# Recurrence of a two-layer hybrid trunk: one chunk's state updates on separate rows of the array, and VectorE's new states moved ahead of a weight split

## The reference, cut to what matters

```python
def _gla_chunk(S, inp):
    q, k, v, logf = inp
    b = jnp.cumsum(logf, axis=2)
    ...
    o = o.reshape(B, H, C, -1) + jnp.einsum('bhck,bhkv->bhcv', q * jnp.exp(b), S)
    b_last = b[:, :, -1]
    S_new = jnp.exp(b_last)[..., None] * S + jnp.einsum(
        'bhck,bhcv->bhkv', k * jnp.exp(b_last[:, :, None] - b), v)
    return S_new, o
```

## Time and profile before

| | |
|---|---|
| time, median of 3 runs | 2693.89 us (2693.68 to 2694.4) |
| the profiled execution's own time | 2695.14 us |
| its span, first to last instruction | 2693.3 us |
| granted TensorE clock, mean | 0.994 |
| one trip of the recurrence loop, heads 0 to 13 finished in it | 31.4 us |
| busy: PE / DVE / ACT / POOL | 98% / 66% / 48% / 15% |

### The profile page before, as it was taken

One profiled execution on the slowest core, in us unless ns is written; L12 is line 12 of the kernel. 1 busy time (PEld: TensorE's weight loads), 2 busy tenths in 40 slices (PEclk: granted clock), 3 DMA queues, 4 the chain that ended last, 5 costly groups with the idle time before them and its releaser, 6 DMA issues.

```text
span 2693.3 us, 55150 instructions
## 1 busy us (share of the span) xinstructions
PE 2649.2 (98%) x19678; PEld 2631.1 (98%) x19678; DVE 1765.3 (66%) x2908; ACT 1300.5 (48%) x2173; POOL 403.6 (15%) x792
## 2 busy tenths in 40 slices
PE   8999999999999999999999999999999999999997
PEld 8999999998999999999999999998999999999997
DVE  7888888847766534666645865548676535767644
ACT  6555666545444433444444566545444333444443
POOL 2111111101322100222200000002322101222200
PEclk9999999999999999999999999999999999999999
DMA  6444444444554555454555422344545555544553
GB/s 231 145 140 135 145 136 133 133 157 137 174 166 161 163 164 169 160 168 159 166 166 168 142 90 89 118 156 141 170 159 169 160 164 165 167 161 166 160 170 115
DMA packets 122671, 413.57 MB, mean 154 GB/s; under 512 B 13856, under 2 KB 20160, under 8 KB 122592
## 3 DMA queue, kind: packets, MB, share of 16 engines
q1 hardware_dynamic: 114480, 406.37, 47.2%
q10 hardware_dynamic: 7056, 3.21, 0.4%
q0 software_dynamic: 1056, 2.92, 0.3%
HBM read 406.97 MB, written 5.48 MB: 153 GB/s over the span
## 4 chain that ended last, share of the span: by engine, by line
PE 96%; DVE 3%; ACT 1%; issue 0%; DMA 0%; DVEq 0%; SPq 0%; ACTq 0%
PE bank L231 30%; PE bank L233 30%; PE bank L232 30%; DVE X L1126 1%; DVE Y L1123 1%; PE bank L1681 1%; PE bank L806 1%; DVE h_lo L1110 1%; DVE w_lo L225 1%; PE bank L767 1%; PE bank L774 0%; PE bank L807 0%; DVE Y L1140 0%; PE bank L1686 0%; ACT w_hi L218 0%
## 5 line engine op out<-in xcount | busy, mean ns | idle before, releaser
L231 PE MATMUL bank<-h_hi,w_hi 128*128 128x288 f32 (+1 forms) x4208 | 1266.4, 301 | 22.5 <-DVE h_lo L1110 13.5
L225 DVE TENSOR_TENSOR w_lo<-raw,w_hi 128x1024 fp32r<-128x1024 f32 (+2 forms) x786 | 955.2, 1225 | 453.7 <-ACT w_hi L218 453.2
L232 PE MATMUL bank<-h_lo,w_hi 128*128 128x288 f32 (+1 forms) x4208 | 1252.6, 298 | 0.0
L233 PE MATMUL bank<-h_hi,w_lo 128*128 128x288 f32 (+1 forms) x4208 | 1248.9, 297 | 0.0
L218 ACT ACTIVATE w_hi<-raw 128x1024 fp32r<-128x1024 f32 (+2 forms) x786 | 808.0, 1037 | 852.3 <-PE bank L233 846.7
L231 PEld LDWEIGHTS bank<-h_hi,w_hi 128*128 128x128 f32 x4208 | 792.9, 188 | 28.2 <-issue 22.6
L233 PEld LDWEIGHTS bank<-h_hi,w_lo 128*128 128x128 f32 x4208 | 796.4, 189 | 0.2
L232 PEld LDWEIGHTS bank<-h_lo,w_hi 128*128 128x128 f32 x4208 | 794.7, 189 | 0.6
L1295 POOL TENSOR_TENSOR ext<-yt,small 128x256 f32<-128x256 f32 x176 | 213.0, 1210 | 1507.4 <-ACT yt L1181 1036.1
L231 PE MATMUL bank<-g_hi,w_hi 128*128 128x288 f32 x1408 | 416.8, 296 | 0.0
L232 PE MATMUL bank<-g_lo,w_hi 128*128 128x288 f32 x1408 | 415.4, 295 | 0.0
(11 more groups left out here) (251 smaller groups left out, 2034.7 us busy)
## 6 DMA issues: line engine op xcount, KB each, us to landing
raw<-in_w_fi SPq DMA_DIRECT2D x352, 512.0 KB, 4.0
raw<-in_w_hi_in SPq DMA_DIRECT2D x128, 512.0 KB, 4.0
raw<-in_w_fo SPq DMA_DIRECT2D x128, 512.0 KB, 3.5
raw<-in_w_fo SPq DMA_DIRECT2D x64, 384.0 KB, 3.3
raw<-in_w_ho SPq DMA_DIRECT2D x32, 512.0 KB, 4.1
raw<-in_w_mo SPq DMA_DIRECT2D x32, 512.0 KB, 3.8
raw<-in_w_down SPq DMA_DIRECT2D x18, 512.0 KB, 4.5
raw<-in_w_ukv SPq DMA_DIRECT2D x16, 512.0 KB, 3.7
```

Source lines behind the costliest of these rows:

```text
L225: dve.tensor_tensor(w_lo[:, ch.slot, 0:n], raw[:, ch.slot, 0:n], w_hi[:, ch.slot, 0:n].bitcast(F32), ALU.subtract).then_inc(lo_done, 1)
L231: pe.matmul(out, w_hi[:, ch.slot, w], rhs_hi, start=start, stop=False)
L232: pe.matmul(out, w_hi[:, ch.slot, w], rhs_lo, start=False, stop=False)
L233: return pe.matmul(out, w_lo[:, ch.slot, w], rhs_hi, start=False, stop=stop)
```

## The change

The products for the third block are restricted to the rows that hold keys: rows 0 to 63 for the prompt, rows 64 to 95 for the sample. The fourth product writes columns 384 to 511 of bank `GS` in place of `SU`, and L614 reads it there. This holds for heads 0 to 14; head 15's updates stay as they are. In the loop, VectorE's `new_states` moves from behind `lo(5)` to before it. The order in the end functions is unchanged.

```diff
@@ new_states
             dve.scalar_tensor_tensor(out=s_new[:, 1, :], in0=s_old[:], scalar=HG.EB[:, T - 1:T],
-                                     in1=su[:, 3 * P:4 * P], op0=ALU.mult, op1=ALU.add)
+                                     in1=(GS if su is SU else su)[:, 3 * P:4 * P], op0=ALU.mult, op1=ALU.add)
@@ hgrn_dve
                 gates_keys_queries(dve, r)
-            lo(5)
             if tail:
                 new_states(dve, t)
+            lo(5)
             if main:
                 decay_sums(dve, r)
@@ updates
-            for n in range(NB + 1):
-                up = pe.matmul(su[:, n * P:(n + 1) * P], ktok[0:BL, n, :], vtok[0:BL, min(n, NB - 1), :], start=True, stop=True)
+            if su is SU:
+
+                rows = [(SU, 0, slice(0, BL)), (SU, 1, slice(0, BL)), (SU, 2, slice(0, 64)), (GS, 3, slice(64, BL))]
+            else:
+                rows = [(su, n, slice(0, BL)) for n in range(NB + 1)]
+            for bank, n, part in rows:
+                up = pe.matmul(bank[:, n * P:(n + 1) * P], ktok[part, n, :], vtok[part, min(n, NB - 1), :], start=True, stop=True)
             up.then_inc(S["updates"], 1)
```

## The result

The changed kernel takes 2699.56 us in the median of 15 runs (2698.78 to 2700.08), the kernel before 2694.59 us in 15 runs (2693.68 to 2696.54). The ratio is 1.0019, 95% interval 1.0012 to 1.0025: 5.0 us or 0.19% slower, just inside the 0.2% that the prediction took for no change, yet with an interval that leaves 1 out. The span of the profiled execution goes from 2693.3 to 2698.3 us at the same granted clock of 0.994.

A forecast was written before the change was run, and what follows sets the result against it. TensorE, busy for 98% of the span, was taken as the bound. The move's -2.5 us plus 8.6 for three changes of size gave +6.1, from 2693.89 to 2700.0 us; range 2692.8 to 2701.3, the forecast's own 2698.8 to 2701.3.

The forecast's parts named there:

- rivals with pairs: In `updates`, the third and fourth products run at once: -0.25 us in sum with the move, 2693.6; chance 0.34.
- part of the price: In `updates`, the fourth product's weights load while the third streams: 0.10 less per head, +4.6 us, 2698.5; chance 0.06.
- Three changes of size, no overlap: In `updates`, TensorE stops entering the third product, entering the fourth and leaving: +0.575 us a head, +8.6; chance 0.54.
- The price of a change: Around the narrow products, idle time plus a weight load with nothing over it: 0.20 us per entry, 0.175 for leaving.
- the way out: From the narrow products to L762's transposes: a stop plus a weight load estimated at 0.75 x 0.10, 0.175 us a head.
- The wait of the outputs: At L774, waiting for L620's states costs 0.21 us a head in twelve heads; the move removes it: -2.5 us.
- The sum of the two parts: The move's -2.5 us plus 8.6 for the third block on separate rows gives +6.1 us, median 2700.0.
- `lo(5)` and its transfer, late by 1.1 us, cost nothing: In the loop, `lo(5)` ends at 268.4 instead of 267.26; covers of 4.5 us for `mm(5)`, 9 us for the transfer.
- The states don't wait for the updates: In VectorE's `new_states`: updates end 1.17 us before L604, delayed by 0.50 at most; the rival wait got no chance.
- What would show it: Signs: no L620 waits at L774, three PEld idle times of 0.17 us, L767 to L762 1.40, trip about 31.77.
- The rules weighed: For `updates`: changing tiling mode drains TensorE (three changes, the choice), or weight loads overlap across differing row groups (pairs).

The follow-up runs named there:

- e3_pair: The changed kernel with the fourth product on rows 64 to 127, the last 32 zeros, so both narrow products have 64 rows; 2693.31 us.
- e6_four_changes: The changed kernel with its four products reordered to 64, 96, 32, 96 rows, giving four changes of size; 2703.68 us.
- e1_move: The kernel before with only `new_states` moved ahead of `lo(5)`, updates and L614 unchanged; 2691.89 us.
- e2_split: The changed kernel with `lo(5)` back ahead of `new_states`, so only the products on separate rows remain; 2699.36 us.
- e4_bank: The changed kernel with all products on 96 rows again, the fourth still in the other bank; 2691.52 us.

## Why the prediction was right, step by step

It gave 2700.0 us, +6.1, inside 2692.8 to 2701.3; measured were 2699.56 and +5.0. The range says little about the mechanism, since it also holds the rivals with pairs (2693.6) and with part of the price (2698.5); the rows and the experiments decide it. That the time came out within 0.4 us while the difference missed by 1.1 is luck: the kernel before took 2694.59 us beside the changed one, 0.7 more than the 2693.89 that the forecast stood on.

- *Three changes of size, no overlap* (chance 0.54): right. e3_pair shows that the size is the reason: in the same banks, and from the same first rows, the products pair as soon as both have 64 rows. Nor is part of the price hidden: the two steps of the fourth product, 266.65 to 267.07, take 0.42 us, as do the two of the third. e6_four_changes and the two kernels with one narrow product show that the price goes with the number of changes. The rival with pairs was the right sum for another kernel: it gave -0.25 us, and e3_pair, which pairs, measured -1.1, lower mostly for the way out that is mis-sized in both sums.
- *The price of a change*: the two entries were 0.19 to 0.20 each, as taken from L1686. The term that was mis-sized is the way out. It was 0.175, with the late load estimated at 0.075; measured are 0.09 for the stop (267.07 to 267.27, less 0.11) and 0.04 over all three transposes (0.29 less 0.24 in the rows; 0.286 less 0.248 read to the nanosecond), 0.13 together. The estimate scaled the load by its columns; why less than that shows before the transposes is open. So the edit cost 0.52 us a head in place of 0.575, 7.8 us in place of 8.6.
- *The wait of the outputs*: -2.5 was forecast and e1_move measured -2.5, by the mechanism named: 0.10 of idle time and 0.11 of a bare weight load in each head. The forecast took twelve heads from the view of waits. In the trace thirteen start late, heads 1 to 13, by 0.05 to 0.13 us and the bare load, 2.65 us in all.
- *The sum of the two parts*: the number came out, but the reasoning behind one term did not hold. The prediction took the move's 2.5 us as a gain of the move. e2_split shows that beside the split the wait goes in either order, since TensorE comes 0.5 us later and the states had held it up by 0.13 at most. The split alone gives +5.0, not +7.6. Either edit removes the wait by itself, so the 2.5 us come off once: beside the split the move adds nothing.
- *`lo(5)` and its transfer, late by 1.1 us, cost nothing*: right; e1_move would have shown it. The transfers of these weights take 4.6 to 4.9 us from issue to landing in every kernel with the move, against 4.0 before and 4.1 in e2_split, so with the move they are longer as well as later; why is open. The cover of 9 us holds the 0.8 us more.
- *The states don't wait for the updates*: right for heads such as 6, where L604 ends at 268.15 and L613 starts at 268.11, and the updates had ended at 267.34 (265.90 + 1.44). It is not right for head 0 and head 14, where VectorE now waits 1.00 and 0.49 us for them:

```profile
77.14 0.29 DVE L613 COPY s_mid<-bank 128x128 f32<-128x128 f32 x1 [1.00 <-PE bank L772]
...
521.35 0.29 DVE L613 COPY s_mid<-bank 128x128 f32<-128x128 f32 x1 [0.49 <-PE bank L772]
```

The prediction gave this no price, and it has none: the outputs of both heads start 0.13 us behind the record before them.

- *What would show it*: 1.40 us from L772 to L762 was expected, 1.37 came. A trip of 31.77 us was expected, 31.71 came. Idle times of 0.17 us marked "issue" on PEld were expected and are not in the view of waits: behind records of 128 columns the idle time is shorter, while behind 288 columns, in e6_four_changes, it is 0.17. The row of weight loads shows 0.13 before the transposes (265.77 + 1.37 to 267.27):

```profile
265.77 1.37 PEld L772 LDWEIGHTS bank<-vtok,ktok 96*128 96x128 f32 x8
267.27 0.28 PEld L762 LDWEIGHTS bank<-ident,row_tiles 128*96 128x96 f32 x3
```

- *The rules weighed*: what the Trainium skill says in "TensorEngine Tiling (Array Packing)", Tiling Modes, that a change of tiling mode and not of tile drains TensorE, is what the traces of e3_pair and of the changed kernel show here, 0.09 to 0.10 us a stop. The rule in the Trainium skill, "TensorE: Matmul & The Clock Gate", Part 3, that weight loads overlap running matmuls when their row groups differ, holds here for 64 rows beside 64 (e3_pair: the records of a pair start within 0.01 us) and not for 32 beside 64 (in the changed kernel the first 32-row record starts 0.20 us behind the last 64-row one).

The fastest version is the move without the split: e1_move at 2691.89 us, with or without the second bank (e4_bank, 2691.52 us), some 8 us under the changed kernel and 2.5 to 2.9 under the one before.

## What to carry to other kernels

In this kernel products on separate rows ran side by side when both had 64 rows, and one after the other when they had 64 and 32. So pad the smaller one with zeros, and count the changes of size around the pair: here two changes cost 0.32 us and one pair of 128-column fp32 products saves 0.22. It would take a longer run of paired products, such as L1686's twelve records, to pay; no run here put that to the test. A wait that is over by 0.1 us can vanish through any delay ahead of it, so measure each part of a change alone before you credit it with a gain. Two edits whose terms are summed need a look at whether the one already removes what the other is for.

## What the runs showed of the hardware that was not expected

A change of row size costs one stop and, behind it, one bare weight load, whatever the direction: the steps at 96 to 64, 64 to 32 and 32 to 128 rows are all 0.20 to 0.21 us where 0.11 is usual, though 64 to 32 goes to rows on which nothing was running. 96-row products beside 128-row ones cost nothing: the steps between them are 0.13 and 0.11 us. And the two records of one fp32 product on rows 0 to 63 and those of the next on rows 64 to 127 seem to interleave: in e3_pair the four start in pairs, at 264.03 and 264.25. The rows do not name the product of a record; but records of `updates` that stand on the same rows start at least 0.11 us apart everywhere else, so each pair should hold one of each product, and the fourth would not wait until the third has ended.
